# Four heads by 32 tokens in a gather, and both parts of a pick summed together on four column groups

## What is computed

```python
q = rms_norm((xb @ wq).reshape(blk, 8, 256), qn_w)         # 8 heads
s1, s2 = q[..., :128] . k1,  q[..., 128:] . k2             # 128 scores each
v1, i1 = top_k(s1, 16);  v2, i2 = top_k(s2, 16)
cand = v1[..., :, None] + v2[..., None, :]                 # 16 x 16
sc, sel = top_k(cand, 16)                                  # 16 picks a head
eidx = take(i1 * 128 + i2, sel);  g = softmax(sc)
act = gelu(einsum('td,thkd->thk', xb, u[eidx]))            # dot with row u
out = einsum('thk,thkd->td', g * act, v[eidx])             # weighted sum of rows v
```

## Time and profile before

| | us |
|---|---|
| median of 3 runs (lowest, highest) | 5161.53 (5159.58, 5164.9) |
| the profiled execution, its own time | 5164.3 |
| its span, first to last instruction | 5162.6 |
| PE busy | 3510.0 (68%) |
| DVE busy | 2785.9 (54%) |
| POOL busy | 1563.8 (30%) |
| ACT busy | 1378.0 (27%) |
| the software DMA queue (gathers): 1107.36 MB | 53.6% of 16 engines |

### The profile page before, as it was taken

One profiled execution on the slowest core, in us unless ns is written; L12 is line 12 of the kernel. 1 busy time (PEld: TensorE's weight loads), 2 busy tenths in 40 slices (PEclk: granted clock), 3 DMA queues, 4 the chain that ended last, 5 costly groups with the idle time before them and its releaser, 6 DMA issues. The chain is left out here.

```text
span 5162.6 us, 43530 instructions
## 1 busy us (share of the span) xinstructions
PE 3510.0 (68%) x13217; PEld 1859.7 (36%) x13217; DVE 2785.9 (54%) x7544; ACT 1378.0 (27%) x4604; POOL 1563.8 (30%) x1191
## 2 busy tenths in 40 slices
PE   4999666665699997875434677769655555555556
PEld 2768553542443345543212244536211111111111
DVE  2350433345445533757665664344677777777775
ACT  1111331012325422322222222032332333332332
POOL 2545000133211121214443332011343444434443
PEclk7999577877799998667777667879777777777778
DMA  5543134368677776559988999466899999999998
GB/s 184 179 155 125 36 106 134 98 204 324 249 269 268 270 287 236 215 214 321 332 317 322 412 385 355 170 235 205 324 417 401 417 415 407 412 414 410 416 413 366
DMA packets 428509, 1473.86 MB, mean 285 GB/s; under 512 B 40785, under 2 KB 166641, under 8 KB 293074
## 3 DMA queue, kind: packets, MB, share of 16 engines
q0 software_dynamic: 152064, 1107.36, 53.6%
q1 hardware_dynamic: 261842, 356.51, 20.7%
q10 hardware_dynamic: 14368, 7.21, 0.5%
HBM read 1403.58 MB, written 74.57 MB: 286 GB/s over the span
## 5 line engine op out<-in xcount | busy, mean ns | idle before, releaser
L2304 PE MATMUL expert_acc<-uv_ring,diag 128*64 128x512 f32 x4096 | 1374.0, 809 | 990.3 <-ACT diag L2249 890.7
L2117 POOL DMA_INDIRECT uv_ring<-in_peer_uv,pick_idx x1056 | 1181.2, 1119 | 2535.5 <-PE expert_acc L2304 1776.6
L2223 DVE SCALAR_TENSOR_TENSOR uv_ring<-uv_ring,n_pairs 128x1024 f32<-128x1024 f32 x1056 | 1278.1, 1226 | 446.3 <-DMA uv_ring<-in_peer_uv,pick_idx 445.1
L2304 PEld LDWEIGHTS expert_acc<-uv_ring,diag 128*64 128x64 f32 x4096 | 316.7, 171 | 1933.4 <-ACT diag L2249 1304.4
L2249 ACT ACTIVATE diag<-half_pattern,pick_weight 128x64 f32<-128x64 f32 x1024 | 298.5, 338 | 598.3 <-DVE pick_weight L2192 587.3
L2258 ACT ACTIVATE gelu_cube<-dots_now 128x2 f32<-128x2 f32 x528 | 106.0, 201 | 1101.7 <-DVE uv_ring L2223 1063.8
L559 PE MATMUL h_acc_q<-in_w_all_q,n_all_q 128*128 128x512 f32 (+1 forms) x800 | 353.5, 597 | 0.0
L2190 DVE SCALAR_TENSOR_TENSOR gelu_now<-gelu_tanh,dots_now 128x2 f32<-128x2 f32 x528 | 85.1, 161 | 380.4 <-ACT gelu_tanh L2261 303.8
L2261 ACT ACTIVATE gelu_tanh<-gelu_cube,dots_now 128x1 f32<-128x1 f32 x1056 | 253.2, 286 | 16.2
L556 PE MATMUL h_acc_q<-n_all_q,in_w_all_q 128*128 128x272 f32 x896 | 213.0, 397 | 18.9 <-DMA in_w_all_q<-in_w_in 18.9
L559 PEld LDWEIGHTS h_acc_q<-in_w_all_q,n_all_q 128*128 128x128 f32 (+1 forms) x800 | 135.7, 174 | 216.5 <-issue 216.5
(11 more groups left out here) (417 smaller groups left out, 5044.8 us busy)
## 6 DMA issues: line engine op xcount, KB each, us to landing
in_w_p<-in_w_in SPq DMA_DIRECT2D x34, 1024.0 KB
in_w_all_q<-in_w_in SPq DMA_DIRECT2D x17, 2048.0 KB
ada_w<-in_w_ada SPq DMA_DIRECT2D x12, 2048.0 KB, 9.3
q_broadcast_q<-qk_rows_dram SPq DMA_DIRECT2D x24, 1024.0 KB, 17.5
uv_ring<-in_peer_uv,pick_idx POOLq DMA_INDIRECT x1056
past_keys_q<-in_cache_kv_g SPq DMA_DIRECT2D x16, 1024.0 KB, 15.7
past_rows_q<-in_cache_kv_g SPq DMA_DIRECT2D x16, 1024.0 KB
score_pair<-scores SPq DMA_DIRECT2D x66, 128.0 KB
```

The source lines that it names most:

```text
L2117: pool.indirect_dma_start(self.ring[:, 2 * slot + s, :], None, self.x["peer_uv"][0], bass.IndirectOffsetOnAxis(ap=self.idx[:, q % 2, s, k: ...
L2223: ins = dve.scalar_tensor_tensor(out=row, in0=row, scalar=1.0, in1=self.n2[:, tile % 2, s if tile < LAST_TILE else 0, :], op0=ALU.mult, op ...
L2304: ins = pe.matmul(self.acc[s * 64:(s + 1) * 64, c, :], self.diag[:, part % DIAGS, s, :], rows, start=first, stop=last)
```

## The change

A gather now holds four heads by 32 tokens. A tile has four such quarters. Part 2k of a group (now four heads) holds pick k of quarters 0 and 1, part 2k+1 pick k of quarters 2 and 3. The number of gathers, parts and bytes gathered is as before. TensorE sums both parts of a pick at once: 8 matmuls, each with 32 columns of weights, which go to four column groups in turn, and it frees two slots at the end. The choice of picks has four units for a group of 32 parts, from part 8 on. The scores of a tile are stored in four DMAs, not two. The rows `n2` of one tile now fill the buffer (16 DMAs, not 4, and twice the bytes): quarters 0 and 1 are loaded when all but the last part of the tile before are through their dots, 2 and 3 when the last one is. The mixer begins after head 4, with four units of picks, not two, before its first part; 6 turns, not 24, lie in the first query phase, and `FRONT_PARTS` is 230, so 298 parts are left for the end.

The diff, cut to its core:

```diff
-    stores = [2 if w == P else 1 for _, w, _ in tiles]
+    stores = [QUARTERS if w == P else 1 for _, w, _ in tiles]
...
-                    for e in range(2):
-                        row = ((at // 64 + e) * PH + h) * 64
-                        sp.dma_start(dram["scores"][row:row + 64, :], stage[e * 64:(e + 1) * 64, n, :])
+                    for e in range(QUARTERS):
+                        row = ((at // S_TOK + e) * PH + h) * S_TOK
+                        sp.dma_start(dram["scores"][row:row + S_TOK, :], stage[e * S_TOK:(e + 1) * S_TOK, n, :])
...
-    FROM = {3: 0, 4: 2, 5: 7, 6: 12, 7: 18, 8: 24}
+    FROM = {5: 0, 6: 2, 7: 4, 8: 6}
...
-        return h in (2, 4, 6)
+        return h == PICK_HEADS
...
-        if h == 2 and name in self.begin:
+        if h == PICK_HEADS and name in self.begin:
...
+QUARTERS = P // S_TOK
+PICK_HEADS = P // S_TOK
+GROUP_PARTS = 2 * TOPK
+PICK_FROM = GROUP_PARTS - 6 * QUARTERS
...
-        self.n2 = keep("n2_pairs", [P, 2, 2, D])
+        self.n2 = keep("n2_quarters", [P, QUARTERS, D])
...
+    def load_n2(self, tile, pair):
+        if tile:
+            sp.wait_ge(self.dots_ready, self.tile_end(tile - 1) - 1 + pair)
+        for quarter in range(2 * pair, 2 * pair + 2):
+            for e in range(PICK_HEADS):
+                at = tile * P + quarter * S_TOK
+                sp.dma_start(self.n2[e * S_TOK:(e + 1) * S_TOK, quarter, :], ...)
...
-        if i < N_PARTS and k == TILE_PARTS - 12:
-            self.load_n2(tile + 1)
+        if k == TILE_PARTS - 1 and tile < LAST_TILE:
+            self.load_n2(tile + 1, 0)
+        if k == 0 and 0 < tile < LAST_TILE:
+            self.load_n2(tile, 1)
...
-            pool.wait_ge(self.picks_ready, 2 * (q + 1))
+            pool.wait_ge(self.picks_ready, q * QUARTERS + quarter + 2)
         at_least(pool, self.part_free, part - PART_SLOTS + 1)
...
-        for s in range(2):
+        for u in range(QUARTERS):
             for step in range(6):
-                self.pick(0, s, step)
+                self.pick(u, step)
...
-        while self.summed < min(i - self.lag, N_PARTS):
-            self.sum_part(self.summed)
-            self.summed += 1
+        while self.summed + 2 <= min(i - self.lag, N_PARTS):
+            self.sum_pick(self.summed)
+            self.summed += 2
...
-        pe.wait_ge(self.diag_ready, part + 1)
+        pe.wait_ge(self.diag_ready, part + 2)
...
         for c in range(2):
-            for s in range(2):
+            for n in range(QUARTERS):
+                k, s = part + n // 2, n % 2
...
-                    ins = pe.matmul(self.acc[s * 64:(s + 1) * 64, c, :], self.diag[:, part % DIAGS, s, :], rows, start=first, stop=last)
+                    ins = pe.matmul(self.acc[n * S_TOK:(n + 1) * S_TOK, c, :], self.diag[:, k % DIAGS, s, :], row, start=first, stop=last)
...
-        ins.then_inc(self.part_free, 1)
+        ins.then_inc(self.part_free, 2)
...
-FRONT_PARTS = 242
+FRONT_PARTS = 230
```

More of the change, by code:

```diff
@@ L2028, in tile_end, with of_part, load_scores @@
         return min((tile + 1) * TILE_PARTS, N_PARTS)
-    def load_scores(self, q, s):
-        if q >= N_GROUPS:
+    @staticmethod
+    def of_part(part):
+        if part >= LAST_TILE * TILE_PARTS:
+            return LAST_GROUP, part - LAST_TILE * TILE_PARTS, 0
+        q, r = divmod(part, GROUP_PARTS)
+        return q, r // 2, r % 2 * 2
+    def load_scores(self, u):
+        if u >= LAST_GROUP * QUARTERS + 2:
             return
         sp = self.nc.sync
[L2036 to L2040, removed]
-        sp = self.nc.sync
-        at_least(sp, self.dots_ready, self.tile_end(tile - 2) if tile >= 2 else 0)
-        for s in range(2):
[L2044 to L2051, removed]
+        q, quarter = divmod(u, QUARTERS)
+        tile, heads = divmod(q, GROUPS_OF_TILE)
+        row = SEQ * PH + quarter * P if q == LAST_GROUP else ((tile * QUARTERS + quarter) * PH + heads * PICK_HEADS) * S_TOK
+        at_least(sp, self.scores_used, u - 1)
+        sp.dma_start(self.score_pair[:, u % 2].rearrange("p a b -> p (a b)"), self.dram["scores"][row:row + P, :]).then_inc(self.scores_in[u % 2], 16)
+    def load_n2(self, tile, pair):
+        sp = self.nc.sync
+        if tile:
[3 more added lines that the diff above has]
+                at = tile * P + quarter * S_TOK
+                sp.dma_start(self.n2[e * S_TOK:(e + 1) * S_TOK, quarter, :], self.dram["n2"][at:at + S_TOK, :]).then_inc(self.n2_in[pair], 16)
+            if tile == LAST_TILE:
+                return
     def load_x1(self, tile):
@@ L2122, in pool_start, with pick @@
             self.pool(i)
-    def pick(self, q, s, step):
+    def pick(self, u, step):
+        if u >= LAST_GROUP * QUARTERS + 2:
+            return
         dve, link = self.nc.vector, self.dve_order.link
+        (q, quarter), s = divmod(u, QUARTERS), u % 2
         pair = self.score_pair[:, s]
@@ L2186, in weigh @@
         dve = self.nc.vector
-        q, k = divmod(part, TOPK)
+        q, k, quarter = self.of_part(part)
         dve.wait_ge(self.gelu_ready, part + 1)
@@ L2238, in act_start @@
     def act_start(self):
-        for s in range(2):
-            self.exps(0, s)
+        for u in range(QUARTERS):
+            self.exps(u)
         self.nc.scalar.wait_ge(self.pattern_ready, 1)
@@ L2287, in pe, with sum_pick @@
     def pe(self, i):
-        while self.summed < min(i - self.lag, N_PARTS):
-            self.sum_part(self.summed)
-            self.summed += 1
-    def sum_part(self, part):
+        while self.summed + 2 <= min(i - self.lag, N_PARTS):
+            self.sum_pick(self.summed)
+            self.summed += 2
+    def sum_pick(self, part):
         pe = self.nc.tensor
         tile = self.of_tile(part)
-        first, last = part == tile * TILE_PARTS, part + 1 == self.tile_end(tile)
-        slot = part % PART_SLOTS
-        pe.wait_ge(self.diag_ready, part + 1)
+        first, last = part == tile * TILE_PARTS, part + 2 == self.tile_end(tile)
+        pe.wait_ge(self.diag_ready, part + 2)
         if first:
@@ L2300, in sum_part @@
         for c in range(2):
-            for s in range(2):
-                rows = self.ring[:, 2 * slot + s, D + c * 512:D + (c + 1) * 512]
+            for n in range(QUARTERS):
+                k, s = part + n // 2, n % 2
+                row = self.ring[:, 2 * (k % PART_SLOTS) + s, D + c * 512:D + (c + 1) * 512]
                 if tile < LAST_TILE:
-                    ins = pe.matmul(self.acc[s * 64:(s + 1) * 64, c, :], self.diag[:, part % DIAGS, s, :], rows, start=first, stop=last)
+                    ins = pe.matmul(self.acc[n * S_TOK:(n + 1) * S_TOK, c, :], self.diag[:, k % DIAGS, s, :], row, start=first, stop=last)
                 else:
-                    ins = pe.matmul(self.acc[0:S_TOK, c, :], self.diag[:, part % DIAGS, s, 0:S_TOK], rows,
-                                    start=first and s == 0, stop=last and s == 1)
-        ins.then_inc(self.part_free, 1)
+                    ins = pe.matmul(self.acc[0:S_TOK, c, :], self.diag[:, k % DIAGS, s, :], row,
+                                    start=first and n == 0, stop=last and n == QUARTERS - 1)
+        ins.then_inc(self.part_free, 2)
 def experts_rest(nc, ph, experts, begin):
```

83 lines of the change are left out of this document (45 added, 38 removed).

## The result

The changed kernel takes 5230.25 us (median of four runs, 5224.24 to 5234.34), the kernel before 5161.73 beside it: ratio 1.0142, 95% interval 1.0125 to 1.0159. It is slower by 69 us, where 48 less were forecast, and above the range. The profiled execution took 5234.34 us, with a span of 5232.4.

A forecast was written before the change was run, and what follows sets the result against it. Limits were taken as TensorE in projection and last query, a chain in HGRN, DMA in attention, merge and the last stage. Terms from projection -55 to last stage +44 summed to -48 us, giving 5114 us, range 5040 to 5190.

The forecast's parts named there:

- The sums: Expert sums on TensorE: a pick's 16 records take 1.92 us at full clock instead of 3.88; projection 55 us shorter.
- rival 4: Expert sums: the four column groups don't overlap, no gain on TensorE, about 5195 us; chance 0.03.
- GpSimd's 239 us of waits for picks: Group borders in the last stage: GpSimd's waits for pick indices fall to near nothing, -45 us.
- Ring slots freed in pairs: Last stage: an even part waits for the next one's weights, gathers start later; costs nothing, margin 1 to 3 us.
- Rival 2: Last stage: pair-wise freeing leaves the DMA queue dry at each of 149 picks; 0.6 us each gives about 5203; chance 0.13.
- HGRN "about half of the chain runs through TensorE, so -18": HGRN: 38 of 75 us of sums saved, about half on the path, so -18 us, bounds 0 and -38.
- n2: Tile borders in the last stage: eight DMAs issued late, DVE stalls 3 to 5 us; +20 us, bounds 0 and +40.
- The stores: Score stores on SP's queue: 5 us more a head; +29 in the first query stage, last query stage -5 net.
- The opening: From the mixer's start to the norm: 196 us instead of 213; taken as -20 us, bounds -60 and +15.
- rival 3: From HGRN through merge: TensorE's clock stays at the lower level, +56 us, about 5170, no gain; chance 0.07.
- Rival 1: HGRN, attention and merge: chains give back the sums' time, half of 173 us, about 5055 in all; chance 0.2.
- Rival 5: Opening and stores cost nothing because SP hides them: -40 and -14 more, 5065 us; chance 0.07.

The follow-up runs named there:

- Experiment 3: Kernel before, but two parts summed together after the weights of both, two slots freed at once; layout, stores and n2 unchanged: 5323.2 us, ratio 1.032.
- experiments 2: Kernel after, but each part summed by itself on two of the four column groups, freeing its one slot: 5200.4 us, ratio 1.0081 to before.
- experiment 5: Kernel after, but sums by pick only until the second span's projection ends, by part from HGRN on: 5155.4 us, ratio 0.9998 to before.
- Experiment 4: Kernel before, with only the first 512 columns of each part's sums made, except at a tile's first and last part: 5098.1 us, ratio 0.9876.
- experiment 1: Kernel after, with a second n2 buffer in the last stage, rows of tiles 4 to 8 loaded 12 parts ahead: 5233.4 us, ratio 1.0137 to before.
- Experiment 8: Kernel before, with a tile's scores stored in four DMAs of 32 rows, not two of 64: 5169.5 us, ratio 1.0016.
- the version with 5105 us: Kernel after, sums by pick until the projection ends, by part from there, projection's spread factor 1.35 in place of 1.0: 5105.2 us, ratio 0.9892 to before.
- the spread alone: Kernel before with only the spread of parts changed, projection's factor 1.35 in place of 1.0, 242 parts in the front: 5132.4 us, ratio 0.9953.

## Why the prediction was wrong

**Right.** The sums: 16 records on four column groups take 1.92 us, as long as 8 on two (rival 4 is out), and the projection fell by 58 where 55 were forecast. The sample tile of the kernel before shows what one group takes, at a clock of 0.97:

```profile
5128.48 3.62 PE L2306 MATMUL expert_acc<-uv_ring,diag 128*32 128x512 f32 x8 [1.28 <-ACT diag L2249]
```

So 16 records would take 7.24 us on one group, and four groups are 3.8 times as fast. The prediction's estimate of 3.2 times and 2.2 us, scaled from the section "Part 3: Packing small matmuls" of the Trainium skill's page "TensorE: Matmul & The Clock Gate", was too slow; this trace shows 1.92 us. GpSimd's 239 us of waits for picks are gone, and eight parts inside a tile take 40.2 us, where the average before was 41.6: over 298 parts (1.4 / 8 x 298) 52 us, against 45 forecast. Attention, branches to norm: as forecast.

**The step that failed: "Ring slots freed in pairs ... So: nothing, but with little to spare".** I costed it at nothing in the last stage and not at all in HGRN, merge and query. Rival 2 put its place in the last stage alone, at each pick. There it is nearly harmless here: 12 us (1594 to 1582). Experiment 3 has 150 us for it in four stages (42, 42, 21, 45) of the old kernel, in its harder form. In the kernel after the part of it that experiments 2 and 5 undo is 12 to 15 us in HGRN, 26 to 28 in merge, 30 or 31 in query, 7 to 12 in the last stage: some 80 us, and experiment 5 is 75 us faster. Two things are seen with it: the odd part's gather starts a turn later, and in the query stage the front's loads come late when gathers come in bursts. How the 80 us divide between the two isn't shown. That a stage is short of no engine, as I read of HGRN, was the warning: a wait can cost much where work is a chain.

**HGRN "about half of the chain runs through TensorE, so -18".** Experiment 4 takes 28 us of its 75 us of sums away and gains 2. Here shorter sums pay where TensorE is the limit. Of the 31 us that HGRN lost, 16 to 19 stay with sums by part (experiments 5 and 2). VectorE is busy 10 us longer there than before in both kernels (183 to 194 and 193), of which 9 are the choice of picks: 152 records of `pick` start in the stage, not 120. Whether that is all of it wasn't tried and stays open. So do the 10 to 12 us that merge keeps in the same two experiments; two more parts lie there, and the loads of `n2` are larger.

**n2: "Loss 5 us a tile, four tiles: +20".** It measured 17.5 a tile, 70 in all; the eights around a border were 4 us over the average before, so the change added some 13. I had counted the stall (3 to 5, measured 19 at the border shown) and the extra bytes at 427 GB/s, 2.5 us. But while 2.1 MB of n2 rows are moved the queues make some 315 GB/s of everything, and experiment 1 shows 12.5 us a tile for it even where nobody waits for the rows. The trace of before had shown this price: 325 GB/s for 24 us in the earlier trace rows, which I had put down to a group's border. But the timeline of before has SP's queue issue a tile's n2 rows just ahead of that stretch, and I had not looked at SP there:

```profile
4297.27 2.37 SPq L2047 DMA_DIRECT2D n_pairs<-n  x4
```

The three group borders in this trace with such a load beside them make 320, 325 and 328 GB/s over 24 us (from 3968, 4304 and 4638), six without one 385 to 403. So the load, of half the size, was the larger part of that dip. The section "Bandwidth" of the Trainium skill's page "DMA: Bandwidth & Descriptors" advises transfers of 1 MiB or more for at least three quarters of the peak. These are of 128 KB, and the lower rate beside them (315 against 423 GB/s) agrees with the direction; whether the size is the reason, no run shows.

**The stores: "a head now takes 23.4 us, then 28.3".** Experiment 8 shows 2 us a head, not 5. The opening came out 35 us better than forecast: the start of the mixer 50 us later instead of 66, and 108 us from there instead of 130. Five heads at 3 us less make 15 of these 38 us; the rest wasn't traced, and my "three heads 74" doesn't follow from 28.3 a head, which makes 85. The five microseconds of TensorE's wait in the earlier trace rows were not all behind the stores. In the last query stage the stores cost nothing; the +31 was the pairs'.

**The clock** (rival 3): it did fall, from 0.68 to 0.54 in merge, but experiment 4, with the same fall and half of the sums, shows that the two together cost nothing there. Rival 1 fell with experiment 4 too: HGRN, attention and merge give back 11 us of the sums' time, where it needed half of the 173. Rival 5 was half right, in the opening.

**Not tried:** a ring of six slots under the sums by pick, which would say whether depth alone cures them, fewer and larger DMAs for the same n2 bytes, and n2 rows brought in once and copied to the other heads on the chip.

## What to carry to other kernels

Packing two buffers' work into one step that frees both is not free for a ring: every second buffer comes free a turn later, and loads go out in bursts. Here that cost some 80 us. Look in every stage, not only the one with the most transfers, for who waits on the ring and what other loads queue behind the burst. Pay for packed sums only where TensorE is full (here the projection), and then move more of that work there: this is the version with 5105 us, 1.1% under the kernel before, when neither the whole change (+1.4%) nor the spread alone (-0.5%) does it. A transfer for which no engine waits can still cost the queues time, and more than its bytes at the best rate: here 12.5 us for 2.1 MB, which are 4.9 us at 427 GB/s.

## What was unexpected of the hardware

While 16 DMAs of 128 KB ran beside the gathers, the 16 DMA engines moved 315 GB/s at a busy share of 1.02, against 423 just before. And with half of the expert sums left out the granted clock of merge fell from 0.68 to 0.52, and the stage, with its queues at a share of 0.96, was no longer than before (436 us, not 444).
